# Moving instructions between places on four engines: SSD slots and the second block's convolution branch

## What is computed

```python
zxbcdt = h @ w_in
z, xbc, dt = jnp.split(zxbcdt, [SSD_D_INNER, SSD_D_INNER + SSD_CONV_DIM], axis=-1)
xbc = jax.nn.silu(causal_depthwise_conv(xbc, conv_w, conv_b))      # 4 taps
xs, b_in, c_in = jnp.split(xbc, ...)
decay = jnp.exp(jnp.where(causal, a_cs[..., :, None] - a_cs[..., None, :], -jnp.inf))
cb = jnp.einsum('bclgn,bcsgn->bcgls', c_c, b_c)
y_diag = jnp.einsum('bcgjls,bcsgjp->bclgjp', cb[:, :, :, None] * decay, xdt)
y = y + xs * d_skip
g = (y * jax.nn.silu(z)).reshape(bsz, L, SSD_GROUPS, ...)
g = g * lax.rsqrt(jnp.mean(g * g, axis=-1, keepdims=True) + EPS)   # per group
```

```python
y_a = neighbourhood_attention(q, k, v, rpb[l]) @ w_attn_branch[l]
y_b = short_gated_conv(cb, cc, ch, conv_w[l]) @ w_conv_branch[l]   # cb * conv3(cc * ch)
merged = jax.nn.sigmoid(ga) * y_a + jax.nn.sigmoid(gb) * y_b
```

## Time and profile before

| | us |
|---|---|
| median of 3 runs | 1112.82 (1112.5 to 1112.93) |
| the profiled execution | 1112.04 |
| its span in the profile | 1110.4 |
| TensorE busy | 1096.2 (99%) |
| VectorE busy | 766.8 (69%) |
| ScalarE busy | 653.5 (59%) |
| GpSimd busy | 165.0 (15%) |
| DMA | 189.96 MB, mean 171 GB/s |

### The profile page before, as it was taken

How to read it: one execution, slowest core, us unless ns; L and a number is a source line. 1 busy time by engine, 2 the same in 40 slices (tenths; PEclk the granted TensorE clock), 3 DMA queues, 4 the chain that set the end, 5 groups by cost and what they waited for, 6 DMA issues and landing times.

```text
span 1110.4 us, 24004 instructions
## 1 busy us (share of the span) xinstructions
PE 1096.2 (99%) x8963; PEld 1067.3 (96%) x8963; DVE 766.8 (69%) x1154; ACT 653.5 (59%) x1075; POOL 165.0 (15%) x152
## 2 busy tenths in 40 slices
PE   9999999999999999999999999999999999999998
PEld 8999999999999999988899999999998999999998
DVE  7988999778565555588686665558787687666543
ACT  7899999655554433577565554446546655555331
POOL 0435434317000000112020000000003201000000
PEclk9999999999999999999999999999999999999999
DMA  6544544585545454443265555555444555555552
GB/s 240 205 157 156 185 153 159 151 260 167 174 171 179 163 187 171 134 136 113 73 213 188 182 187 181 181 195 172 152 151 144 182 181 187 183 189 188 182 182 91
DMA packets 53226, 189.96 MB, mean 171 GB/s; under 512 B 5920, under 2 KB 7200, under 8 KB 53168
## 3 DMA queue, kind: packets, MB, share of 16 engines
q1 hardware_dynamic: 51408, 182.59, 48.5%
q0 software_dynamic: 1760, 6.59, 1.9%
HBM read 188.07 MB, written 1.08 MB: 170 GB/s over the span
## 4 chain that ended last, share of the span: by engine, by line
PE 70%; DVE 14%; ACT 9%; issue 4%; DMA 2%; ACTq 0%; POOL 0%; DVEq 0%; SPq 0%
PE lin L462 22%; PE lin L464 22%; PE lin L463 22%; DVE w_lo L1426 4%; ACT w_hi L947 3%; DMA w_raw<-w 2%; DVE cv L1533 1%; ACT cv L1038 1%; ACT ee L1062 1%; DVE sg L1543 1%; ACT sg L1021 1%; ACT dd L1052 1%; DVE s_m L1836 1%; ACT sg L1019 1%; ACT pr L1347 1%
## 5 line engine op out<-in xcount | busy, mean ns | idle before, releaser
L1426 DVE TENSOR_TENSOR w_lo<-w_raw,w_hi 128x1024 fp32r<-128x1024 f32 (+3 forms) x318 | 382.2, 1204 | 252.6 <-ACT w_hi L947 251.9
L947 ACT ACTIVATE w_hi<-w_raw 128x1024 fp32r<-128x1024 f32 (+2 forms) x342 | 351.9, 1034 | 225.6 <-PE lin L464 212.9
L462 PE MATMUL lin<-x_hi,w_hi 128*128 128x256 f32 (+1 forms) x1504 | 432.3, 287 | 3.0 <-DVE cv L1533 2.4
L464 PE MATMUL lin<-x_hi,w_lo 128*128 128x256 f32 (+1 forms) x1504 | 428.4, 285 | 0.0
L463 PE MATMUL lin<-x_lo,w_hi 128*128 128x256 f32 (+1 forms) x1504 | 427.4, 284 | 0.0
L462 PEld LDWEIGHTS lin<-x_hi,w_hi 128*128 128x128 f32 x1504 | 283.6, 189 | 5.9 <-issue 3.6
L464 PEld LDWEIGHTS lin<-x_hi,w_lo 128*128 128x128 f32 x1504 | 283.8, 189 | 0.0
L463 PEld LDWEIGHTS lin<-x_lo,w_hi 128*128 128x128 f32 x1504 | 283.0, 188 | 0.5
L464 PE MATMUL lin<-hid_hi,w_lo 128*128 128x256 f32 (+1 forms) x768 | 218.2, 284 | 0.0
L463 PE MATMUL lin<-hid_lo,w_hi 128*128 128x256 f32 (+1 forms) x768 | 217.9, 284 | 0.0
L462 PE MATMUL lin<-hid_hi,w_hi 128*128 128x256 f32 (+1 forms) x768 | 217.4, 283 | 0.0
(11 more groups left out here) (302 smaller groups left out, 1506.0 us busy)
## 6 DMA issues: line engine op xcount, KB each, us to landing
w_raw<-w SPq DMA_DIRECT2D x342, 512.0 KB, 3.2
acs_bc<-acs_dram POOLq DMA_DIRECT2D x8, 544.0 KB, 4.9
bias_mask<-rpb POOLq DMA_DIRECT2D x4, 512.0 KB, 10.1
h<-h SPq DMA_DIRECT2D x4, 272.0 KB, 3.8
out<-h SPq DMA_DIRECT2D x8, 128.0 KB, 3.1
cst<-const SPq DMA_DIRECT2D x1, 808.0 KB, 6.8
vecs<-vec SPq DMA_DIRECT2D x1, 131.5 KB, 2.2
w_raw<-w SPq DMA_DIRECT2D x1, 128.0 KB, 5.4
```

What stands on the lines that cost most here:

```text
L462: mm3(o, wh, xh, start=first and i == 0, stop=False)
L464: ins = mm3(o, wl, xh, start=False, stop=last and i == kts - 1)
L947: a(w_hi[pg.slot][:, 0:n], w_raw[pg.slot][:, 0:n], ACT.Copy).then_inc(w_hi_done, pages)
L1426: tt(w_lo[pg.slot][:, 0:n], w_raw[pg.slot][:, 0:n], w_hi[pg.slot][:, 0:n].bitcast(F32), ALU.subtract)\
```

## The change

Six moves; nothing is added to the arithmetic and nothing is taken away.

1. ScalarE, slots: `conv0(s, 0)` and both pages of chunk c+2 go ahead of z's sigmoid.
2. VectorE, slots: the low half of page 0 of chunk c+2 goes from ahead of the causal product to behind `conv(s, 0)`.
3. GpSimd, slots: the first low half goes between y2 and `y_sum`; the DMA of the decays for slot s+1 is issued in slot s, ahead of the last low half.
4. TensorE, slots: `group_stat` goes between the two tiles of chunk c+2; the wait for the bank (`free`) goes ahead of it.
5. VectorE, second block: the copy of the transposed weights goes from behind the second low half of step i-1 to the start of step i.
6. Second block: `yb`, `yb_hi` and `yb_lo` go from steps 10 and 11 to steps 11 and 12, and `yb` to the start of its step.

```diff
                     lin_chunk(c + 1, k + 1, T, 0 if first else None)
-                if has_stat:
-                    group_stat(s + (-2))
-                if has_lin:
-                    lin_chunk(c + 2, k + 2, T)
+                    free(k + 2)
+                    for j in range(2):
+                        tile(lin[:, 2 * (k + 2).parity + j, 0:T], (c + 2).page(j), x_hi, x_lo, T).then_inc(w_used, 1)
+                        if has_stat and j == 0:
+                            group_stat(s + (-2))
...
                     decay(g, 1)
+                if has_lin:
+                    conv0(s, 0)
+                    hi((c + 2).page(0))
+                    hi((c + 2).page(1))
+                if has_scan:
                     kz = g.times(3, K_GRP + 2)
                     act.wait_ge(drained[kz.parity], kz.half + 1)
                     sigmoid(z_sg[:, :, :], zg_step, g.times(3), z_raw[:, :, :])
-                if has_lin:
-                    hi((c + 2).page(0))
-                    conv0(s, 0)
-                    hi((c + 2).page(1))
...
                 if has_lin:
-                    lo((c + 2).page(0))
                     if has_scan:
                         causal_cb(g)
                     conv(s, 0)
+                    lo((c + 2).page(0))
                     clamp(sg[:, 0:2, :], cv[:, 0:2, :]).then_inc(clamped, 1)
...
             for i in range(20):
                 c, k = At(C_IN2 + i), At(K_IN2 + i)
+                if 8 <= i < 16:
+                    dve.wait_ge(pT2_done, i - 7)
+                    if i >= 10:
+                        dve.wait_ge(pv2_done, 2 * ((i - 8) // 2))
+                    nc.vector.tensor_copy(p_t2[i % 2][:, :], ps7[:, :]).then_inc(pt2_done, 1)
+                if i in (11, 12):
+                    j = i - 11
+                    dve.wait_ge(drained[(k + (-1)).parity], (k + (-1)).half + 1)
+                    dve.wait_ge(cv2_step, 8)
+                    tt(yb[:, 2 * j:2 * j + 2, :], cv2[:, 2 * j:2 * j + 2, :], cb_r[:, 2 * j:2 * j + 2, :], ALU.mult)\
+                        .then_inc(yb_done, 1)
                 lo((c + 2).page(0))
...
-            def slot(s, has_lin=True, has_stat=True):
+            def slot(s, has_lin=True, has_stat=True, has_rows=True):
                 c, gs = s.times(3, C_GRP), s + (-2)
-                if has_lin and s.base:
-                    acs_rows(s)
...
                     tt(y2[:, :, :], y1[:, :, :], z_s[gs.parity][:, :, :], ALU.mult).then_inc(y2_done, 1)
+                if has_lin:
+                    lo((c + 2).page(1))
+                if has_stat:
                     pool.wait_ge(ysq_done, (gs + 1).value)
                     tt(y_sum[:, :], h_sq[:, 0, :], h_sq[:, 1, :], ALU.add).then_inc(ysum_done, 1)
                 if has_lin:
-
-                    lo((c + 2).page(1))
                     lo((c + 3).page(1))
+                    if has_rows:
+                        acs_rows(s + 1)
                     lo((c + 4).page(1))
```

More of the change, by code:

```diff
@@ L1394, in _ @@
                     exps2(i - 6)
-                if i in (10, 11):
-                    j = i - 10
+                if i in (11, 12):
+                    j = i - 11
                     act.wait_ge(yb_done, j + 1)
@@ L1952, in _ @@
                 lo((c + 2).page(1))
[L1953 to L1957, removed]
                 if i == 0:
@@ L2098, in _ @@
             lo(At(C_GRP + 4).page(1))
+            acs_rows(At(1))
             slot(At(1), has_stat=False)
@@ L2103, in _ @@
             slot(At(6))
-            slot(At(7))
+            slot(At(7), has_rows=False)
             slot(At(8), has_lin=False)
```

## The result

| | before | after |
|---|---|---|
| runs beside each other, median us | 1112.66 (1112.48 to 1112.93, 4 runs) | 1105.12 (1104.70 to 1105.91, 4 runs) |
| profiled execution, us | 1112.04 | 1105.25 |
| its span, us | 1110.4 | 1103.6 |

The ratio is 0.9933, with a 95% interval of 0.9916 to 0.9950: the change makes the kernel 0.7% faster. 1106.0 was forecast for the median, 1103.6 for the span. The medians lie 7.5 apart and the profiled spans 6.8: the profiled execution of the kernel before is 0.6 under its median, that of the changed kernel 0.1 over. The forecast's sum is of spans, and it is compared with the spans.

A forecast was written before the change was run, and what follows sets the result against it. TensorE, busy 1096.2 of 1110.4 us, was taken as the bound, so only its idle time could be won. Slot ends 3.2 + tail 0.9 + second block 2.7 = 6.8, median 1112.82 to 1106.0 (span 1103.6), own range 1104.6 to 1107.4.

The forecast's parts named there:

- The ring of ScalarE and VectorE: SSD slots: page, low half, convolution, clamp and sigmoid, not passing TensorE, set the 22.67 us period (13.84 + 5.93 + 2.90).
- TensorE's own pace of 22.2: SSD slots: period without the 0.48 us lost per slot, 22.67 - 0.48; predicted after the change.
- the late weights of the second block: Second block: TensorE waits 2.9 us in three waits for VectorE's softmax weights `pr`.
- Slots, steps 1 to 4: SSD slots: reordered ScalarE and VectorE work meets TensorE's pace; six slot ends save 3.2 us, bounds 0 and 3.2.
- the blocked clamp: SSD slots: VectorE's clamp takes 1.63 us because GpSimd's page is running; forecast 0.4 after the change.
- Step 5: SSD slots, TensorE: the group sum's matmul, moved 3.1 us later between the third chunk's tiles, costs what it did.
- Tail: After the slots: waits for `y_sum` and `g_lo` go, with refilling; saves 0.9 us, bounds 0 and 0.9.
- Block, steps 1 to 3: Second block: waits for `pr` go, 3.2 us, less a new 0.5 stall for the copy: 2.7, bounds 0 and 3.2.
- A: Rival, second block: the late copy stops the value products at four places; gain 0.7 instead of 2.7, 1108.0; 14 in 100.
- B: Rival, slots: a ring of 22.5 remains; slots and tail gain 1.0 instead of 4.1, 1109.1; 14 in 100.
- C: Rival, slots' third chunk: GpSimd's page holds VectorE's low half, 1.3 us wait in each of seven slots; 1115.9; 6 in 100.
- D: Rival, whole change: each wait is replaced by one as long, nothing gained; 1112.5; 6 in 100.

The follow-up runs named there:

- e3: Kernel before with ScalarE's slot order alone (first taps and both pages ahead of z's sigmoid): 1113.53 us, one profiled execution.
- e4: Kernel before with VectorE's slot order alone (low half behind the convolution): 1119.00 us, one profiled execution.
- e5: Kernel before with GpSimd's order alone (third chunk's page ahead of `y_sum`, DMA of `acs_bc` a page earlier): 1109.66 us, one profiled execution.
- e12: Changed kernel with GpSimd's order put back as it was before: 1109.15 us, ratio 0.9970 to the kernel before.
- e10: Changed kernel with `yb`, its rounding and `yb_lo` moved to the block's steps 16 and 17, behind the softmax: 1105.84 us, ratio 0.9937 to the kernel before.
- e8: Kernel before with only the copy of transposed weights moved, to the head of the step: 1111.21 us, one profiled execution.
- e11: Changed kernel with ScalarE's and VectorE's slot order put back as before: 1106.12 us, ratio 0.9938 to the kernel before.

## Why the prediction was right

It was right in sum (6.8 forecast, 6.8 in the span) and in both halves: 4.1 up to the second block, 2.7 in it. The ring of ScalarE and VectorE, TensorE's own pace of 22.2 under it and the late weights of the second block are what the runs show. The slots' gain didn't depend on knowing which edit opens the ring: whatever brings it under 22.2 gives the same period. By its steps:

- **Slots, steps 1 to 4.** Forecast 3.2. Of the 3.84 won in the column of the slots, some 0.5 are the tail's wait for `y_sum`, so the slot ends gave 3.3. In the slot quoted above, times from 144.55: taps at +6.57 (ScalarE idle 0.96; 1.3 forecast), convolution done at +10.3 (+10.3), low half done at +13.1 (+12.8), clamp at +14.0 (+13.9), ScalarE's wait 0.24 (0.3), `y_sum` done at +13.7 (+13.6), the second pair's convolution at +21.2 (+21.1). The low half has 0.8 to spare instead of 1.1, because GpSimd's page ran until +12.0, not +11.6.
- **What those steps did not say** is which edit counts, and there my reading was wrong, as e3, e4 and e5 show. I had taken the blocked clamp for a detail of the ring (a part of its 5.93) and the moves on ScalarE and VectorE for the cure. The 1.2 by which GpSimd's page stretches the clamp is what lifts the ring over TensorE's 22.2, and GpSimd's order alone removes it. ScalarE's and VectorE's moves give about 0.9 on top, in the first two slots, and without GpSimd's they give 0.2 in sum, no more than that column scatters (e12): most slots get shorter, and the two whose clamp is caught give it back. That the total came out all the same is luck in this respect: the change held the edit that matters, and its reasons named another.
- **Step 5**, the group sum: free in its new place, as forecast; left where it was it would have cost about 0.9.
- **Tail.** Forecast 0.9; it is 0.8: some 0.5 in the slots' column and 0.27 behind, the latter no more than that column scatters. That the wait of 0.28 for `g_lo` is gone stands in the list, and nothing took its place.
- **Block, steps 1 to 3.** Forecast 2.7, measured 2.70. With 4.1 less for the earlier start, the weights of step 11 were forecast at 826.3 and `yb_lo` behind them started at 826.27, the copy behind step 12 at 835.05 and it ended at 835.08. The stall behind it was forecast as 0.5 and costs 0.72; e10's wait-free block puts the old stalls at 45.55 - 42.13 = 3.42, where I had 3.2. Both were too small by 0.2, the hand-over and refilling of the waits; that the two cancel is luck.

**Rivals.** A (copy only shifts the stall) is refuted as a whole, yet it is what e8 does with the copy's part: 2.0 of waits for `p_t`. B (a ring of 22.5 remains) is refuted for the change, 22.20; e12 has the same loss by another way, six slots of 22.5 on average of which four stay under 22.4. C was told as 6 in 100 for the whole change; e4 shows that its mechanism is real: with VectorE's order alone the slots are 6.8 longer, some 5.4 without the stretch at the lower clock. The Trainium skill's rule in SBUF — State Buffer, section Who interferes with whom, that the engine that issues first holds the shared way into memory for its whole instruction, fits the low half's three lengths: page 0.10 ahead, 3.36; page 0.84 ahead, 2.67; no operation of GpSimd running, 1.23. The prediction named the clamp as its example; the clamp has one input in SBUF, and the low halves are the two-input case. D is refuted.

## What to carry to other kernels

A loop's ring can pass through an instruction that is long only because another engine's is running: before rearranging the ring, look whether what stretches an instruction in it can be moved. Edits to such an order don't add up one by one: two that cost or give nothing alone gave 0.9 here beside a third, so each should be run alone as well as taken back alone. And one slot isn't all slots: in e12 the steady loop has slots of two kinds, and the wait followed from the kind that is rarer. In this softmax pipeline a last stall of 0.7 stayed where the foreign work moved by one step, and went where it moved behind the softmax.

## What the runs showed of the hardware

VectorE's operations that read only SBUF and GpSimd's took turns in every row read here, and in both directions, which I had priced for VectorE only: 1.23 becomes 2.03, 2.67 or 3.36 by the moment of the start (low half), 0.44 becomes 1.01, 1.63, 1.80 or 2.63 (clamp, one input), 2.01 becomes 3.23 (`mm`), and on GpSimd `y_sum` goes from 0.77 to 1.66 and a page from 2.38 to 3.38. The convolution, which reads PSUM beside SBUF and runs through the same stretches, takes 2.51 in e3, e11 and e12 as in the kernel before, and ScalarE's rows keep their lengths.

The longest of these collisions stands in nearly every slot with `g_lo` in every kernel, the changed one too. `g_lo` (two instructions) with GpSimd's page running, in a slot, and without it, in the tail, both in the kernel before:

```profile
129.06 3.04 DVE L1577 SCALAR_TENSOR_TENSOR g_lo<-z_s,vecs,g_hi 128x272 f32 x2
...
208.58 0.92 DVE L1577 SCALAR_TENSOR_TENSOR g_lo<-z_s,vecs,g_hi 128x272 fp32r<-128x272 f32 x2 [0.59 <-ACT g_hi L1103]
```

That is 2.1 a slot, more than the clamp's 1.2, and it costs no time in the steady slot of the earlier trace rows, since VectorE stands idle 1.67 behind it before its low half. It also means that VectorE's busy share holds time in which it was held up.
